# The first tile's norm takes its gain and bias by channel, behind the transposes, and four residual products move behind the first head's queries

## The reference

```python
h = layer_norm_2(DN_ALPHA * h + mix, ln_mix_g[i], ln_mix_b[i])
ffn = peer_ffn(h, peer_w_q[i], peer_sub_keys[i], peer_u[i], peer_v[i])
h = layer_norm_2(DN_ALPHA * h + ffn, ln_ffn_g[i], ln_ffn_b[i])

def layer_norm_2(x, g, b):
    ...
    return ((xf - mu) * lax.rsqrt(var + LN_EPS) * g + b)

def peer_ffn(x, w_q, sub_keys, u, v):     # per block of 128 tokens
    q = (xb @ w_q).reshape(128, 8, 2, 128)
    s = jnp.einsum('thcd,hckd->thck', q, sub_keys)
    ...                                   # top 16 of 128 per side, top 16 of the 256 pairs
    h = jax.nn.gelu(jnp.einsum('thkd,td->thk', u[eidx], xb), approximate=False)
    return jnp.einsum('thk,thkd->td', gate * h, v[eidx])
```

## Time and profile before

| what | value |
|---|---|
| median of 3 runs | 2270.11 us (2269.82 to 2270.64) |
| the profiled execution's own time | 2269.78 us |
| its span | 2268.0 us |
| PE busy | 2068.8 us (91%) |
| DVE busy | 1443.0 us (64%) |
| ACT busy | 698.2 us (31%) |
| POOL busy | 714.4 us (31%) |
| first gather of the first layer issued | 827.95 us |
| first gather of the second layer issued | 1604.28 us |

### The profile page before, as it was taken

One profiled execution on the slowest core, in us unless ns is written; L12 is line 12 of the kernel. 1 busy time (PEld: TensorE's weight loads), 2 busy tenths in 40 slices (PEclk: granted clock), 3 DMA queues, 4 the chain that ended last, 5 costly groups with the idle time before them and its releaser, 6 DMA issues.

```text
span 2268.0 us, 21464 instructions
## 1 busy us (share of the span) xinstructions
PE 2068.8 (91%) x6088; PEld 1087.8 (48%) x6088; DVE 1443.0 (64%) x3261; ACT 698.2 (31%) x1515; POOL 714.4 (31%) x627
## 2 busy tenths in 40 slices
PE   9999999999999999999887878799999988787876
PEld 8864445455867655444332222266554444222222
DVE  2989777675551356666666666532766666667664
ACT  1012102111200214344433434423334344433442
POOL 1152420000000014454454445300254455444442
PEclk9999999999999999999999999999999999999999
DMA  5444444444545359999999999963799999999997
GB/s 223 156 148 176 167 160 139 171 169 162 193 160 221 113 232 370 421 422 421 422 421 422 422 422 421 422 261 150 281 422 421 421 421 422 421 422 421 422 421 316
DMA packets 98443, 703.07 MB, mean 310 GB/s; under 512 B 11136, under 2 KB 11648, under 8 KB 13248
## 3 DMA queue, kind: packets, MB, share of 16 engines
q0 software_dynamic: 73856, 537.17, 57.1%
q1 hardware_dynamic: 20016, 141.04, 17.3%
q10 hardware_dynamic: 4496, 23.92, 2.7%
HBM read 700.51 MB, written 1.05 MB: 309 GB/s over the span
## 4 chain that ended last, share of the span: by engine, by line
PE 44%; DMA 30%; ACT 5%; issue 4%; DVE 2%; POOL 1%; POOLq 0%; DVEq 0%; ACTq 0%
DMA arena<-uv,expert_index 30%; PE aux L1019 14%; PE acc L573 8%; PE acc L538 7%; PE aux L538 5%; PE aux L857 3%; PE acc L1036 2%; PE acc L938 1%; ACT arena L1549 1%; ACT arena L1552 1%; ACT L1549 1%; ACT L1541 1%; POOL arena L1290 1%; DVE arena L2277 1%; PE acc L904 1%
## 5 line engine op out<-in xcount | busy, mean ns | idle before, releaser
L1019 PE MATMUL aux<-arena 128*128 128x512 f32 x2048 | 1005.1, 620 | 181.0 <-ACT arena L1552 177.5
L1290 POOL DMA_INDIRECT arena<-uv,expert_index x512 | 601.0, 1174 | 975.0 <-PE aux L1019 582.8
L2277 DVE SCALAR_TENSOR_TENSOR arena<-arena 128x1024 f32<-128x1024 f32 x512 | 633.2, 1237 | 413.3 <-DMA arena<-uv,expert_index 413.2
L1019 PEld LDWEIGHTS aux<-arena 128*128 128x128 f32 x2048 | 368.3, 193 | 719.2 <-ACT arena L1552 427.5
L1549 ACT ACTIVATE arena<-ident,dots 128x128 f32<-128x128 f32 x512 | 205.3, 401 | 695.2 <-DVE arena L2277 692.9
L573 PE MATMUL acc<-x,w_ring 128*128 128x256 f32 x1264 | 275.8, 381 | 2.5 <-DVE x L1719 2.3
L573 PEld LDWEIGHTS acc<-x,w_ring 128*128 128x128 f32 x1264 | 241.0, 191 | 36.2 <-DVE x L1719 2.5
L1552 ACT ACTIVATE arena<-arena,gate 128x128 f32<-128x128 f32 x512 | 205.5, 401 | 17.1
L1761 DVE TENSOR_TENSOR first_query_weights<-w_ring 128x1024 f32<-128x1024 f32 (+1 forms) x71 | 85.8, 1208 | 101.0 <-PE aux L538 90.3
L538 PE MATMUL acc<-first_query_weights,arena 128*128 128x512 f32 (+1 forms) x284 | 141.6, 581 | 0.1
L1803 DVE SCALAR_TENSOR_TENSOR arena<-arena,channel_vectors (+1 forms) x240 | 108.6, 533 | 0.2
(11 more groups left out here) (324 smaller groups left out, 1896.4 us busy)
## 6 DMA issues: line engine op xcount, KB each, us to landing
w_ring<-stream SPq DMA_DIRECT2D x133, 1024.0 KB, 4.8
arena<-uv,expert_index POOLq DMA_INDIRECT x512, 14.8
arena<-first_heads ACTq DMA_DIRECT2D x6, 1024.0 KB, 8.9
first_query_weights<-first_heads ACTq DMA_DIRECT2D x4, 1024.0 KB, 10.0
row_vectors<-rows ACTq DMA_DIRECT2D x3, 1024.0 KB, 12.1
scratch<-keys ACTq DMA_DIRECT2D x2, 1024.0 KB, 5.6
arena<-ret_out_held ACTq DMA_DIRECT2D x2, 1024.0 KB, 14.8
x<-first_heads ACTq DMA_DIRECT2D x2, 1024.0 KB, 4.8
```

Of the source, the lines that this page charges most:

```text
L1019: last = nc.tensor.matmul(AUX[2 * tt + c][:, :], DG[:, slot, :], G[:, row(layer, slot), D + c * 512:D + (c + 1) * 512], start=False, stop= ...
L1290: pool.indirect_dma_start(G[:, row(layer, s % RING), :], None, uv, bass.IndirectOffsetOnAxis(ap=EIDX[:, par, s:s + 1], axis=0),).then_inc( ...
L2277: v.scalar_tensor_tensor(G[:, row(layer, slot), 0:D], G[:, row(layer, slot), 0:D], 1.0, HTM[:, tt, :], ALU.mult, ALU.mult, accum_out=HD[:, ...
```

## The change

The gain and bias of the mixer's norm are also kept by channel, as 32 more columns of the tile `channel_vectors`. For the first tile of each layer VectorE now writes only (bank - mean) * reciprocal, and the piece with the gain (L2326) falls away. The turned banks are stored in eight pieces of 128 columns with gain and bias applied, k = 0 to 3 by ScalarE and k = 4 to 7 by VectorE, and the queries wait for each k by itself. After that VectorE gives `HTM` its gain and bias with two operations on 1,024 columns, for the dots and the residual of the tile, and tells it by `tokens_gained`. On TensorE `add_residual(1, 1)` moves from ahead of the transposes to behind the first queries, where one product of `rest` stood. On ScalarE the wait for `residual_added` and the third head's transfer move behind `store_turned(0, 0)`. The second tile's norm stays as it was.

```diff
-         ("freq_mla", 1), ("sign", 1), ("half", 2)]
+         ("freq_mla", 1), ("sign", 1), ("half", 2), ("mix_g", 16), ("mix_b", 16)]
...
                 add_residual(0, 1, False)
-                add_residual(1, 1, False).then_inc(residual_added, 1)
                 turn_tokens(0, 0, 4 * layer + 1, True)
                 turn_tokens(0, 1, 4 * layer + 2)
                 pe.wait_ge(early_loaded, 32 * (layer + 1))
 
                 def turned_there(k):
-                    if k % 4 == 0:
-                        ring.wait_stored(uses + k // 4)
+                    pe.wait_ge(turned_dve if k >= KT // 2 else turned_act, KT // 2 * layer + k % (KT // 2) + 1)
 
                 first_queries(turned_there)
-                some(1)
+                add_residual(1, 1, False).then_inc(residual_added, 1)
...
-                pe.wait_ge(tokens_ready, 4 * layer + 2)
+                pe.wait_ge(tokens_gained, layer + 1)
...
                 root(RT)
+                act.sem_inc(diag_ready, 1)
+
+                ring.wait_full()
+                for k in range(KT // 2):
+                    last = nc.scalar.activation(X0[:, k, 0:P], ring.bank()[:, k * P:(k + 1) * P], ACT.Identity,
+                                                bias=col("mix_b", KT * layer + k), scale=col("mix_g", KT * layer + k))
+                    if k < KT // 2 - 1:
+                        last.then_inc(turned_act, 1)
+                ring.release(last)
+                ring.wait_stored(ring.n - 1)
+                act.sem_inc(turned_act, 1)
+                ring.n += 1
+                store_turned(0, 0)
                 act.wait_ge(residual_added, layer + 1)
                 act.dma_start(X1W, first_heads[EARLY * layer + 2]).then_inc(third_loaded, 16)
-                act.sem_inc(diag_ready, 1)
-                store_tokens(0, 0)
-                store_tokens(0, 1)
-                store_turned(0, 0)
...
-                        norm_piece(p, tt, MIX1 if layer else RO, tokens_ready)
+                        norm_piece(p, tt, (MIX1 if layer else RO) if tt else None, tokens_ready)
...
                 mixer_norm(0)
+
+                ring.wait_full()
+                for k in range(KT // 2, KT):
+                    j = k - KT // 2
+                    last = v.tensor_scalar(X0[:, k, 0:P], ring.bank()[:, j * P:(j + 1) * P], col("mix_g", KT * layer + k),
+                                           col("mix_b", KT * layer + k), ALU.mult, ALU.add)
+                    if j < KT // 2 - 1:
+                        last.then_inc(turned_dve, 1)
+                ring.release(last)
+                ring.wait_stored(ring.n - 1)
+                dve.sem_inc(turned_dve, 1)
+                vectors = MIX1 if layer else RO
+                link(v.tensor_tensor(HTM[:, 0, :], HTM[:, 0, :], vectors[:, 0, :], ALU.mult))
+                link(v.tensor_tensor(HTM[:, 0, :], HTM[:, 0, :], vectors[:, 1, :], ALU.add))
+                dve.sem_inc(tokens_gained, 1)
+                ring.n += 1
```

More of the change, by code:

```diff
@@ L405, in build @@
         projected = sem("projected")
-        tokens_ready = sem("tokens_ready")
+        tokens_ready, tokens_gained = sem("tokens_ready"), sem("tokens_gained")
+        turned_act, turned_dve = sem("turned_act"), sem("turned_dve")
         held_loaded = sem("held_loaded")
@@ L2120, in peer @@
             def peer(layer):
-                ring.n += 3
+                ring.n += 1
                 dve.wait_ge(iota_ready, 1)
@@ L2559, in _layout @@
         "half": (np.arange(P)[:, None] // 64 == np.arange(2)[None, :]).astype(np.float32),
+        "mix_g": np.concatenate([chan(a) for a in f("ln_mix_g_2")], axis=1),
+        "mix_b": np.concatenate([chan(a) for a in f("ln_mix_b_2")], axis=1),
     }
```

## The result

| kernel | median | runs | lowest to highest |
|---|---|---|---|
| before | 2269.83 us | 20 | 2266.93 to 2270.86 |
| changed | 2274.22 us | 20 | 2272.20 to 2276.82 |

The ratio is 1.0023 with a 95% interval of 1.0017 to 1.0029: the changed kernel is slower by 0.23%. The measured median is 2.9 us above the upper end of the range. Its profiled execution has a span of 2272.6 us against 2268.0, 4.6 us more, so the two traces hold the difference.

What follows compares the result with a forecast made beforehand. DMA engines bound the gather loops; the change moves only their start, set by TensorE's list in the first layer and the first gather in the second. +0.4 - 0.5 = -0.1 us gave 2270.0 us, range 2268.7 to 2271.3.

Steps and rivals of the forecast that it cites:

- The 32 columns: Load of the added channel-vector columns: 16 KB, 0.04 us at 420 GB/s beside other loads, costing nothing.
- the sentence of the first part: Gather loops fill most of both layers at 420 to 422 GB/s; the change does not touch them.
- C: Rival: third head's transfer collides with the first gathers, 2.5 us per layer, +5.0 us, 2275.1 us; chance 0.04.
- g: Time by which the first queries end earlier, taken the same in both layers: about 0.5 us, bounds 0 to about 1.0.
- the start of group k = 3: First queries: ScalarE's last piece ends 817.62, TensorE starts 0.28 us later at 817.90; 13 steps, 3.1 us, follow.
- The sum 0.89 - g: First layer, TensorE's list: 0.89 us of residual products moved behind the queries, less the earlier queries' end: +0.4 us.
- Rival A: Both layers follow the first gather, so the first layer gains too: -1.0 us, 2269.1 us; chance 0.15.
- B: Rival: the store's pieces eat the gain; +1.3 us, 2271.4, if queries wait for the whole bank; chance 0.18.
- Here an earlier first head counts in full: Second layer, ahead of the gather loop: landing and restart both move with the first gather, -0.5 us.
- my sign of being wrong: Second layer: the prediction is wrong if the eighth gather, forecast near 1628.4, does not move with the first.
- with streamed weights between them: Second layer: seven gathers ahead of the eighth, 17.5 us of transfers from 1604.28, interleaved with weights, keep DMA mostly busy.
- VectorE's two new operations: Gain and bias on 1,024 columns, 1.2 us each, done about 820.6 before scores near 822.3: cost nothing.

Runs made afterwards that it cites:

- the changed kernel at the old place: Changed kernel plus an unused 128-byte tile, gathered rows again 96 bytes behind a multiple of 256: 2269.12 us against 2268.25, ratio 1.0003.
- the norm part alone: Changed kernel with all eight residual products ahead of the transposes, third head's transfer at its old place, rows at 96 bytes: one execution, 2270.56 us.
- the order part alone: Kernel before with four residual products and the third head's transfer moved behind the first queries, norm as before: one execution, 2270.11 us.
- the four kernels at 0: Gathered rows at a multiple of 256 bytes by unused tiles: three with the old order, ratios 0.9938, 0.9933, 0.9927 to before; the changed kernel, 0.9931.

## Why the prediction was wrong

**The step that failed** is the last of the change's parts: "*The 32 columns* are 16 KB, 0.04 us at 420 GB/s, beside other loads: nothing." I costed their load and not what they push. With it falls the sentence of the first part, that the change does not touch the loops. The shift of 128 bytes alone gives 1.0028, and the changed kernel at the old place gives 1.0003. None of my rivals named it; C ended near the measured time, at 2275.1 us, but by a mechanism that did not occur. In the first layer the third head's transfer is issued at 819.89 and lands 5.1 us later, before the first gather is issued; in the second it is issued at 1600.12, and in the three us ahead of 1607.25, before the gathers' data come, the DMA engines move 8 GB/s. The loss sits in the rate of the loops, in both alike (2.54 and 2.40 us).

**g.** Forecast 0.5, measured 0.68 in the first layer. The term that was mis-sized is the start of group k = 3. Behind the leading products, I had ScalarE's last piece end at 817.62 - 812.82 = 4.80 us and TensorE begin that group 0.28 us later, at 5.08. The last piece ended at 814.20 + 1.50 - 810.99 = 4.71 us, and the 13 steps that follow (3.1 us in all), counted back from the end at 7.98, put the start of the group at 4.89, 0.18 us behind the piece. The pieces did cost something: the queries took 4.11 us, 0.30 more than before. The sum 0.89 - g held to the hundredth: +0.21 us. Rival A is refuted by this, and so is B, which needed a g near 0 or below.

**The second layer.** "Here an earlier first head counts in full" failed. It was my sign of being wrong that the eighth gather does not move with the first, and that is what happened. VectorE's gap of 0.51 us inside the search left the first gather only 0.28 us earlier. But the gap is not the reason for the late eighth gather: in the norm part alone the first gather is 0.49 us late and the eighth only 0.08 to 0.16. What I let pass is in the words "with streamed weights between them": the product that opens the way for the next weight block moved one place back on TensorE's list, so the block was issued 0.67 us later by the same count. In the order part alone, with the first gather where it was and the block 1.35 us later, the eighth gather is 0.47 to 0.55 us late. The traces show the time in the DMA engines. In the three us from 16 to 19 behind the second statistics operation they move 276 GB/s before, 246 in the changed kernel, 257 in the norm part alone and 208 in the order part alone. An estimate from this: 68 GB/s less over 3 us are 0.20 MB, or 0.48 us at 422 GB/s, for the order part, and 0.21 us for the changed kernel, against 0.55 and 0.28 us measured. That makes the block the likely cause. It was not moved by itself: the order part also moves the residual products and the third head's transfer.

At equal place the second layer's head is 0.04 to 0.34 us later in the changed order: 39.32 against 39.20 and 39.28 at 96 bytes, 39.48 against 39.29 at 224, 39.36 against 39.02 to 39.15 at 0. So all of the reordering is about +0.25 to +0.55 us by the traces, where I had forecast -0.1; the measured times can't tell this from nothing.

**Small slips.** Three sums of the prediction are off without changing it: 817.67 - (816.32 + 1.21) is 0.14 and not 0.13 us, 818.10 plus two operations is 820.5 and not 820.6, and A and B at g = 0 with half a us of spread give 2268.6 to 2271.5 us, a little wider than the stated range. The measured time lies outside either.

**What held.** The second four transposes began 0.04 us after the first four were done, released by VectorE; the pieces took 1.50 and 1.37 us; VectorE's two new operations and the third head's transfer were hidden; the first layer is bound by TensorE's list and an earlier first gather gives nothing there.

## What to carry to other kernels

Before costing what an edit does, ask what it moves in memory: a table that grew by 128 bytes shifted each tile allocated behind it here, and with the DMA engines as the bound the place of their rows was part of the kernel. Where gathers bound a kernel, try their destination at a multiple of 256 bytes, and compare an edit only at an equal place; here, with rows of 8 KB, that was worth 0.6 to 0.7%, more than the edit that was being judged. If a loop that an edit leaves alone changes its GB/s at a full DMA share, test the place first, with an unused tile.

## What the runs showed that I had not expected

The rate has three levels by the place of the rows within 256 bytes (427, 421 to 422, 420 GB/s), and the steps are small beside the rate itself. GpSimd's issues were longer where the transfers were fastest. All its issues in the kernel with rows at a multiple of 256 (shortest, median, longest, ns):

```profile
L1291 POOL DMA_INDIRECT arena<-uv,expert_index x512: 932/1309/1989, 826.3 to 2224.2; - x171
```

and with rows at 224:

```profile
L1291 POOL DMA_INDIRECT arena<-uv,expert_index x512: 932/939/1992, 826.3 to 2247.4; - x171
```

The median went from 939 to 1309 ns with the same instructions. It is 1228 to 1309 ns in the four kernels at 0 and 937 to 939 in the ten others. No cost shows: in the second layer's window of the kernel at 0 GpSimd is busy 335 of 575 us. Why the issues grow is open. And VectorE's gap of 0.5 us between a copy and the maximum behind it shows in the second layer of every kernel that has the norm part, and in none that lacks it, though the instructions are the same; its cause is open.
